# Sparse attention in order of token blocks, with eight packed query tiles

## The reference

```python
dots = jnp.einsum('bqhd,bkd->bqhk', qib, ki, preferred_element_type=F32)
iscore = jnp.einsum('bqhk,bqh->bqk', jax.nn.relu(dots), wib.astype(F32))
iscore = jnp.where(admissible[None], iscore, -jnp.inf)
_, sel = lax.top_k(iscore, topk)
...
s = jnp.einsum('bqhd,bqkd->bhqk', qb, k_sel, preferred_element_type=F32) * scale
s = jnp.where(valid[:, None], s, -jnp.inf)
p = jax.nn.softmax(s, axis=-1)
return jnp.einsum('bhqk,bqkd->bqhd', p.astype(v.dtype), v_sel)
```

## Time and profile before

| | |
|---|---|
| median of 3 runs | 2704.7 us (2702.99 to 2723.24) |
| profiled execution | 2717.66 us, span 2715.9 us |
| PE busy | 2532.6 us, 93% of the span |
| DVE busy | 1254.2 us, 46% |
| ACT busy | 1078.4 us, 40% |
| POOL busy | 366.4 us, 13% |
| dsa stage, first score to turn stage | 568.5 to 703.2 us of the span |

### The profile page before, as it was taken

The page is one execution under the profiler, slowest core; times in us unless marked ns, Lnnn a source line. Parts: engine busy times, 40 slices in busy tenths (PEclk is TensorE's granted clock), DMA queues, the critical chain, the costliest instruction groups (busy, mean ns, idle before and its releaser), DMA issues. The chain is left out here.

```text
span 2715.9 us, 30590 instructions
## 1 busy us (share of the span) xinstructions
PE 2532.6 (93%) x12099; PEld 2119.4 (78%) x12099; DVE 1254.2 (46%) x2002; ACT 1078.4 (40%) x1601; POOL 366.4 (13%) x188
## 2 busy tenths in 40 slices
PE   4889979989799999999999979996999999999998
PEld 3668658889687888888887767895878888888877
DVE  4464668866443333333337634443433333334365
ACT  4344777766432222222336522443322222222254
POOL 1111104311001222221000011000012222220000
PEclk8999989999899999999999989656999999999999
DMA  4101100000331111111436520004311111113375
GB/s 126 39 16 47 32 16 24 25 1 2 109 117 47 47 48 54 47 47 47 132 94 234 177 70 24 1 1 109 117 47 47 47 49 52 47 47 118 99 243 176
DMA packets 163465, 191.42 MB, mean 70 GB/s; under 512 B 11284, under 2 KB 132468, under 8 KB 163324
## 3 DMA queue, kind: packets, MB, share of 16 engines
q1 hardware_dynamic: 158016, 171.46, 20.6%
q10 hardware_dynamic: 5308, 18.01, 1.7%
HBM read 172.64 MB, written 16.81 MB: 70 GB/s over the span
## 5 line engine op out<-in xcount | busy, mean ns | idle before, releaser
L128 PE MATMUL l_ps<-rest_hi,l_whi 128*128 128x512 f32 x1408 | 439.7, 390 | 4.7 <-DVE rest_lo L1892 4.7
L128 PE MATMUL l_ps<-rest_lo,l_whi 128*128 128x512 f32 x1408 | 439.6, 390 | 0.0
L128 PE MATMUL l_ps<-rest_hi,l_wlo 128*128 128x512 f32 x1408 | 439.1, 389 | 0.0
L1759 POOL TENSOR_TENSOR l_wlo<-l_raw,l_whi 128x1024 fp32r<-128x1024 f32 x88 | 213.1, 2421 | 982.3 <-ACT l_whi L1678 982.3
L128 PEld LDWEIGHTS l_ps<-rest_hi,l_whi 128*128 128x128 f32 x1408 | 264.6, 188 | 60.0 <-DVE rest_lo L1892 5.2
L128 PEld LDWEIGHTS l_ps<-rest_hi,l_wlo 128*128 128x128 f32 x1408 | 264.7, 188 | 55.1
L128 PEld LDWEIGHTS l_ps<-rest_lo,l_whi 128*128 128x128 f32 x1408 | 264.7, 188 | 55.0
L1678 ACT ACTIVATE l_whi<-l_raw 128x1024 fp32r<-128x1024 f32 x156 | 164.2, 1052 | 129.3 <-PE l_ps L128 119.0
L1898 DVE SCALAR_TENSOR_TENSOR l_y_v<-l_ps,main_conv,l_y_v 128x1023 f32<-128x1023 f32 x44 | 56.4, 1283 | 337.7 <-ACT l_y_v L1712 337.7
L1712 ACT ACTIVATE l_y_g<-l_ps,main_conv 128x1024 f32<-128x1024 f32 x44 | 53.1, 1207 | 382.4 <-PE l_ps L128 382.4
L1898 DVE SCALAR_TENSOR_TENSOR l_y_g<-l_ps,main_conv,l_y_g 128x1023 f32<-128x1023 f32 x44 | 56.5, 1283 | 282.9 <-ACT l_y_g L1712 282.9
(11 more groups left out here) (319 smaller groups left out, 4784.6 us busy)
## 6 DMA issues: line engine op xcount, KB each, us to landing
l_raw<-in_ffn_w_in SPq DMA_DIRECT2D x88, 512.0 KB, 3.9
l_raw<-in_ffn_w_out SPq DMA_DIRECT2D x68, 512.0 KB, 3.9
l_rawl<-in_ffn_w_out SPq DMA_DIRECT2D x44, 512.0 KB, 4.2
front_raw<-in_even_w_in SPq DMA_DIRECT2D x20, 512.0 KB, 3.6
l_rawe<-in_ffn_w_out SPq DMA_DIRECT2D x20, 512.0 KB, 3.7
odd_raw<-in_odd_w_qkv SPq DMA_DIRECT2D x10, 512.0 KB, 4.0
setup_xin<-in_x SPq DMA_DIRECT2D x8, 512.0 KB, 11.1
fox_negc<-negc_dram SPq DMA_DIRECT2D x8, 512.0 KB, 3.8
```

The source lines that it names most:

```text
L128: mm = pe.matmul(o, w, m, start=a, stop=z)
L1759: pool.tensor_tensor(wlo[u % 3][:], raw_up[u % 2][:], whi[u % 3][:].bitcast(F32), ALU.subtract).then_inc(up_lo, 1)
```

## The change

The list of steps of the dsa stage runs over blocks 7 down to 0 outside and over the eight heads inside. `causal_stage` tells the two orders apart by whether `keys` is given (`by_blocks`). By blocks it holds eight packed query tiles instead of two, one for each head; ACT packs heads 0 and 1 at the start and head h+2 before it goes on with part h, h = 0 to 5, without a wait; PE waits for a head's packing at its first step, which is step h. The result of a group of four steps is written as four heads of one block. The fox stage goes by heads as before.

```diff
--- before.py
+++ after.py
@@ -1215,7 +1215,9 @@
 
         low = st.sb("low", [P, ROWS, 2])
         rs = st.sb("rs", [P, ROWS])
-        q = [st.sb(f"q{s}", [P, T], F32R) for s in range(2)]
+        by_blocks = keys is not None
+        nq = len(heads) if by_blocks else 2
+        q = [st.sb(f"q{s}", [P, T], F32R) for s in range(nq)]
         nkeys = 2 if keys is None else len(keys)
         k_hi = [st.sb(f"k_hi{s}", [P, T], F32R) for s in range(nkeys)]
         k_lo = [st.sb(f"k_lo{s}", [P, T], F32R) for s in range(nkeys)]
@@ -1238,13 +1240,13 @@
 
         def pack_head_hi(act, h):
             x, r, k = heads[h]
-            if h >= 2:
+            if h >= nq:
                 act.wait_ge(S_ready, last[TB * (h - 1) - 1] + 1)
             if keys is None:
                 own, other = halves(r)
                 act.activation(k_hi[h % 2][own, :], k[own, :], ACT.Copy)
                 act.activation(k_hi[h % 2][other, :], k[own, :], ACT.Copy)
-            pack_hi(act, q[h % 2], x, r).then_inc(hi_packed, 1)
+            pack_hi(act, q[h % nq], x, r).then_inc(hi_packed, 1)
 
         def pack_head_lo(engine, h):
             x, r, k = heads[h]
@@ -1257,10 +1259,10 @@
                     engine.tensor_tensor(k_lo[h % 2][to, :], k[own, :], k_hi[h % 2][own, :].bitcast(F32),
                                          ALU.subtract).then_inc(k_lo_packed, 1)
                     engine.wait_ge(k_lo_packed, 2 * h + i + 1)
-            pack_lo(engine, q[h % 2], x, r).then_inc(lo_packed, 1)
-
-
-        packing = {first[TB * h] - AHEAD + 1: h + 1 for h in range(1, HEADS - 1)}
+            pack_lo(engine, q[h % nq], x, r).then_inc(lo_packed, 1)
+
+
+        packing = {h: h + 2 for h in range(HEADS - 2)} if by_blocks else {first[TB * h] - AHEAD + 1: h + 1 for h in range(1, HEADS - 1)}
 
         def wait_copied(eng, j):
             if j + 1 > dve_upto[j]:
@@ -1287,7 +1289,7 @@
                 def scores(j):
                     n, c, e = parts[j]
                     h, b, ks = steps[n]["h"], steps[n]["b"], key_slot(steps[n]["h"])
-                    if j == first[TB * h]:
+                    if j == first[h if by_blocks else TB * h]:
                         pe.wait_ge(lo_packed, h + 1)
                     if j == 0 and keys is not None:
                         pe.wait_ge(key_lo, 2 * nkeys)
@@ -1295,7 +1297,7 @@
                         pe.wait_ge(mask_ready, 2)
                     if j >= RING:
                         pe.wait_ge(S_taken, j - RING + 1)
-                    out, queries = S[j % RING][:, 0:e - c], q[h % 2][:, b * P:(b + 1) * P]
+                    out, queries = S[j % RING][:, 0:e - c], q[h % nq][:, b * P:(b + 1) * P]
                     pe.matmul(out, queries, k_hi[ks][:, c:e], start=True, stop=False)
                     if forget and e == steps[n]["nk"]:
                         pe.matmul(S[j % RING][:, e - c - P:e - c], mask_id[:], mask[:], start=False, stop=False)
@@ -1394,8 +1396,9 @@
                     inv = rs[:, r:r + GRP].rearrange("p (s c) -> p s c", c=1)
                     dve.reciprocal(inv, sums[:, :, HD:HD + 1]).then_inc(rs_ready, 1)
                     dve.wait_ge(rs_ready, grp + 1)
-                    dve.tensor_tensor(o_tm[:, x["b"]:x["b"] + GRP, x["col"]:x["col"] + HD], sums[:, :, 0:HD],
-                                      inv.to_broadcast([P, GRP, HD]), ALU.mult).then_inc(O_taken, 1)
+                    into = (o_tm[:, x["b"], x["col"]:x["col"] + GRP * HD].rearrange("p (s c) -> p s c", c=HD) if by_blocks
+                            else o_tm[:, x["b"]:x["b"] + GRP, x["col"]:x["col"] + HD])
+                    dve.tensor_tensor(into, sums[:, :, 0:HD], inv.to_broadcast([P, GRP, HD]), ALU.mult).then_inc(O_taken, 1)
 
                 for i in range(0 if keys is None else nkeys):
                     dve.wait_ge(key_hi, 2 * i + 2)
@@ -2034,7 +2037,7 @@
                                   else isc[:, packed(b)])
             steps = [dict(h=h, b=b, nk=(b + 1) * P, col=h * HD, v=lambda kt: dv[:, kt, :],
                           bias=dsa_bias(b))
-                     for h in range(NH) for b in range(TB)]
+                     for b in reversed(range(TB)) for h in range(NH)]
             heads = [(dq[:, h // 2, :], h % 2, 0) for h in range(NH)]
             o_dsa = o.sb("o_dsa", [P, TB, D // 2], side="right")
             causal_stage(nc, g, "dsa", heads, [kk[HD:P, :]], [slice(HD, P)], steps, o_dsa)
```

## The result

The changed kernel takes 2718.69 us (median of 20 executions, 2706.88 to 2729.25), the kernel before 2710.9 us (20 executions, 2697.95 to 2723.24). The ratio is 1.0043 with a 95% interval of 1.0028 to 1.0059: on 2711 us that is 11.7 us slower, 7.6 to 16. The two medians by themselves are 7.8 us apart, also inside that interval. The forecast was 10 us.

The account below looks back on a forecast made before the run. PE was taken to bound the sparse-attention stage. Start 7.8, narrow blocks 1.2 and drain 1.0 us sum to 10 us more, on a median of 2704.7: 2714.7 us, range 2705 to 2731.

Parts of the forecast that it names:

- What bounds the stage: Sparse-attention stage: PE is the bound from its second head on; DVE and ACT have slack.
- the prices per part: PE time for scores, turn and values of one part: 1.80 us at 512 keys, 0.90 at 256, 0.53 at 128.
- The start: First eight steps: waits for newly packed query tiles, 6.0 us idle plus 1.8 us for low clock; bounds 6.0 and 10.
- The three waits: At the stage's start PE idles for POOL's packing of heads 1, 2 and 3: 0.85, 0.75 and 4.4 us.
- forecast for the clock: After the long wait PE restarts at half clock for 4.5 us; 4.2 us more at low clock, 1.8 us lost.
- The narrow blocks: Steps of blocks 1 and 0 in a row: ACT bounds block 0, 1.2 us lost; bounds 0 and 6.
- The drain: Stage end: the last five parts have no scores beside them, about 1.0 us more idling; bounds -0.6 and +2.
- A: Rival: after the start's long wait the clock stays low for the remaining stage, 94 us, near 2808; chance 5%.
- B: Rival: longer start chain between ACT, POOL and PE, narrow steps at their latency, 2721 to 2731 us; chance 15%.
- C: Rival: packing runs further ahead of PE at the start, block order costs 0 to 4 us, 2705 to 2709; chance 15%.
- D: Rival: a gain from the 1.2 us at the stage's end and the start's low clock, at most 2702; chance 4%.
- What the profile would show: Three start waits, POOL's packings within 25 us, PE then full until block 0, stage about 145 us, other stages unchanged.

Follow-up runs that it names:

- the experiment (0.55): Blocks 3 to 0 stepped by heads, against the block-order kernel with ACT packing all upper halves first and DVE head 1's lower half: stage 135.4 us, 0.55 less.
- the kernel by heads with preparation: Kernel before, order of heads, with POOL preparing the sparse stage's keys and head 0's query tile in the fox stage: ratio 0.9996 of before.
- the one by blocks: Block order with that fox-stage preparation, ACT packing all upper halves first, DVE head 1's lower half: ratio 1.0022 against the kernel before.

## Why the prediction was right

*What bounds the stage.* Right. PE fully busy before and after from the moment the packing is through; the prices per part held to the hundredth. A step of block 0 beside a turn and values of 256 keys should take 0.20 + 0.22 + 0.44 = 0.86, and does:

```profile
702.10 0.31 PE L1301 MATMUL dsa_S<-dsa_k_hi,dsa_q 128*128 128x128 f32 x1
...
702.96 0.31 PE L1301 MATMUL dsa_S<-dsa_k_hi,dsa_q 128*128 128x128 f32 x1
...
709.11 0.28 PE L1312 MATMUL dsa_TR<-main_const,dsa_prob 128*128 128x128 f32 x1
...
709.56 0.28 PE L1312 MATMUL dsa_TR<-main_const,dsa_prob 128*128 128x128 f32 x1
```

*The start, 7.8 us forecast.* Until 585.52 the changed kernel has issued eight parts of scores, three turns and one of values, 6.04 us of work by the prices, in 16.73 us. The kernel before would have these 6.04 us of work done in 6.3 + 2.4 = 8.7 us (3.6 of it at low clock). The loss is 8.0 us. The three waits are at the places given, and the three restarts came at 571.31, 573.83 and 580.94, each 0.3 to 0.5 us later than walked, of which 0.3 is the stage's own later start. The profile's rows give 0.44 + 0.45 + 4.18 = 5.1 us of idling and not 6.0. A part of that is how it counts: the last matmul ahead of the first wait (570.24) is busy for 0.63 us by its modelled end, where such matmuls follow each other at 0.43, so this wait is shown about 0.2 us short; if all three are, 5.7 are left of the 6.0. The experiments give this item its parts: 5.6 us for the late packing of head 3 with its share of the clock, of which 1.9 go away if PE is merely kept at work (forecast for the clock: 1.8), and 2.0 for the two short waits (137.9 to 135.95). With both repaired 1.2 us stay, of which the narrow steps' order explains 0.55.

*The narrow blocks, 1.2 us forecast.* Wrong in size: nothing was lost while scores were still issued (PE 5.00 of 5.00 from 703 to 708). The term set ACT's 0.68 us against 0.53 for a whole narrow part. But PE's turns and values lag five and seven parts behind the scores, so for the first narrow scores PE still has wider parts, 0.75 to 0.86 us a step, and of the eight steps of block 0 only those in the drain have ACT as the bound.

*The drain, 1.0 us.* There the loss is: steps at a distance of 0.45 us where PE needs 0.33. The term had ACT's whole 0.68 us in each of the last steps, exponential and copy. Drain and narrow steps were forecast at 2.2 us and are 0.6, by the prices (125.6 us from 585.52 to the end of the last values where 125.0 are the work) and by the experiment (0.55).

*The sum.* 10 forecast, 8.6 by these parts, 8.8 measured on the stage. The 11.7 of the whole times has an interval that holds it; that the remaining 2.9 us are anything but scatter was not shown. Some of the closeness is luck. The end was forecast at 2.2 us and is 0.6, which the start's 8.0 for 7.8 doesn't make up for, so the sum is 1.2 us too high against the stage; the ratio of whole times happens to lie on its other side. The forecast of the time itself, 2714.7, was 4.0 us below the 2718.69 measured, mostly because it stood on a median of three runs, 2704.7, where that of twenty is 2710.9. And the counterpart of the profiled execution was put at 2728 us and came out at 2715.67, as the part behind the stage was 11 us shorter in it.

*The rivals.* A (the clock stays low): it came back 4.6 us after the restart, where 4.5 was taken, in steps with 512-wide scores. The odd layer's stretch at 0.50, on which it rested, wasn't a fixed state either (in the first two of its twelve windows PE was busy for 7.55 and 9.75 us and not for 10): in the second profile of before the same stretch had 0.65 on average. B (longer chain, serial narrow steps): no. C (the start is hidden): no in the changed kernel, but what it assumed, that ACT packs head 3 ahead of copy 0, came true only in the repair that packs all upper halves first, and that gave 5.6 us. D (a gain): no.

*What the profile would show.* All of it came, but for the 0.15 us a step in block 0. The later stages' lengths did change, and the prediction had named that as a sign of being wrong, the odd layer by name. The second profiles show that it isn't one: the part behind the stage differs by 13 us between two executions of the same kernel.

## What to carry to other kernels

Where every step of a new order needs a prepared operand of its own, walk the first steps through each engine's list by hand: the price is set by the entry that stands behind another engine's result, here the packing of head 3 behind copy 0, and not by the sum of the work. Order steps so that the first are the longest, and put preparations that wait for nothing ahead of the first that waits. A stall also costs the clock behind it, here 1.9 us for a wait of 4.2; and changes of a few us are read from the stage's own length, since whole times of this kernel scatter by 25.

## What the runs showed of the hardware

- The granted clock of a busy PE differs between executions at the same place: in the odd layer the matmuls of line 873 went over 137.9 us at 0.53 or over 121.1 us at 0.65, in two profiles of one kernel. In the fox stage the same 13 us were at 1.00 in one kernel's profile and at 0.50 in another's with the same code there; that stretch was 4.6 us longer. Much of the scatter of this kernel's whole time can come from such places; how much was not measured.
- A wait of only 1.23 us of PE, at a change of stages, was followed by half clock (0.50 from 563.8 to 567.0) in the kernel by heads with preparation. In the one by blocks the same wait of 1.23 us was followed by full clock, until PE had idled for another 1.19 us and restarted at 572.80; its window:

```profile
570.45:572.60 2.15, 1.15 (x4) 0.64 (x4) 1.08 (x1) 2.10 (x3) 0.00 (x0) 1.00 0.00 0
```

- In the long wait of the changed kernel the clock stayed at half and PE restarted at 0.56; filled with needless transposes for 3.05 us, the same wait saw the clock rise (0.85 over the 4.2 us).
- Idle PE can be cheaper when filled: 20 needless transposes made the changed stage 1.9 us shorter.
- DVE instructions beside POOL's took up to four times as long (623 to 2450 ns), one with a single input among them.
